# Branch outputs rewritten on gates finished in the projection, with a router on turned tokens and an early start of the first expert

## The reference, cut to what matters

```python
proj = h @ p['w_in'][l] + p['b_in'][l]      # dz and mo are 1024 columns each of it
...
o_dn = o_f + flip(o_b)                      # 8 heads of 128
y_a = (rmsnorm(o_dn, p['dn_onorm'][l]) * jax.nn.silu(dz.reshape(bsz, t, DN_HEADS, DN_DV).astype(f32)))
...
h_ml = h_f + flip(h_b)                      # 4 heads of 256
y_b = rmsnorm(h_ml, p['ml_onorm'][l]) * jax.nn.sigmoid(mo.reshape(bsz, t, ML_HEADS, ML_DV).astype(f32))
y = jax.nn.sigmoid(ga) * (y_a @ p['w_up_a'][l]) + jax.nn.sigmoid(gb) * (y_b @ p['w_up_b'][l])
y = y @ p['w_out'][l]
...
aff = jax.nn.softmax((h @ w_router).astype(jnp.float32), axis=-1)      # 16 experts
gate, idx = lax.top_k(jnp.swapaxes(aff, 1, 2), cap)                    # 16 + 64 tokens each
xe = h[bi, idx]
a = jnp.einsum('becd,edf->becf', xe, w_gate)
u = jnp.einsum('becd,edf->becf', xe, w_up)
ye = jnp.einsum('becf,efd->becd', jax.nn.silu(a) * u, w_down) * gate[..., None].astype(h.dtype)
```

## Time and profile before

| | |
|---|---|
| median of 3 runs | 3671.08 us (3667.51 to 3673.53) |
| the profiled execution | 3677.44 us |
| its span | 3675.6 us |
| mean granted clock of TensorE | 0.953 of full speed |
| projection | 0 to 1391.6 us |
| DeltaNet | 1400.0 to 1755.3 us |
| mLSTM | 1755.8 to 1914.0 us |
| branch outputs | 1915.9 to 1973.5 us |
| merge, without the router tail | 1973.8 to 2454.2 us |
| router tail | 2454.2 to 2522.3 us |
| experts | 2522.6 to 3675.6 us |

### The profile page before, as it was taken

One profiled execution on the slowest core, in us unless ns is written; L12 is line 12 of the kernel. 1 busy time (PEld: TensorE's weight loads), 2 busy tenths in 40 slices (PEclk: granted clock), 3 DMA queues, 4 the chain that ended last, 5 costly groups with the idle time before them and its releaser, 6 DMA issues. The chain is left out here.

```text
span 3675.6 us, 49680 instructions
## 1 busy us (share of the span) xinstructions
PE 3365.8 (92%) x19747; PEld 2764.0 (75%) x19747; DVE 2379.5 (65%) x2580; ACT 1749.4 (48%) x2121; POOL 305.6 (8%) x320
## 2 busy tenths in 40 slices
PE   5899999999999997999665999996999999999994
PEld 0799998888888997889544998874666666666663
DVE  1577456655565664555577334466888888888886
ACT  2444223323323334655323223443777777777774
POOL 0000000000000003241100100000010010010001
PEclk8999999999999998999887999986999999999997
DMA  9322325566663322211342533575999999999997
GB/s 414 132 91 95 125 76 192 206 205 211 208 209 119 113 104 66 69 34 34 81 109 98 176 112 138 217 294 187 372 394 381 399 385 388 399 381 394 397 377 290
DMA packets 181120, 796.74 MB, mean 217 GB/s; under 512 B 17492, under 2 KB 75092, under 8 KB 101604
## 3 DMA queue, kind: packets, MB, share of 16 engines
q1 hardware_dynamic: 162772, 701.71, 51.4%
q0 software_dynamic: 17328, 87.63, 7.1%
q10 hardware_dynamic: 864, 5.27, 0.3%
HBM read 732.10 MB, written 62.46 MB: 216 GB/s over the span
## 5 line engine op out<-in xcount | busy, mean ns | idle before, releaser
L2390 DVE TENSOR_TENSOR expert_lo<-expert_ring,expert_hi 128x2048 fp32r<-128x2048 f32 x384 | 879.4, 2291 | 159.1 <-ACT expert_hi L2327 155.7
L2327 ACT ACTIVATE expert_hi<-expert_ring 128x2048 fp32r<-128x2048 f32 x384 | 735.9, 1917 | 251.2 <-PE bank L2274 228.5
L2272 PE MATMUL bank<-expert_hi,xeT_hi 128*80 128x512 f32 x1024 | 403.8, 394 | 1.2 <-DVE xeT_lo L2395 1.2
L2273 PE MATMUL bank<-expert_lo,xeT_hi 128*80 128x512 f32 x1024 | 402.0, 393 | 0.0
L2274 PE MATMUL bank<-expert_hi,xeT_lo 128*80 128x512 f32 x1024 | 399.2, 390 | 0.0
L451 PE MATMUL bank<-h_hi,part_hi 128*128 128x320 f32 x960 | 302.0, 315 | 6.7 <-DVE part_lo_b L829 3.7
L451 PE MATMUL bank<-h_lo,part_hi 128*128 128x320 f32 x960 | 298.9, 311 | 0.0
L658 ACT ACTIVATE part_hi<-part_x 128x1024 fp32r<-128x1024 f32 x120 | 127.4, 1062 | 247.5 <-PE bank L451 232.8
L1895 ACT ACTIVATE merge_w_hi<-merge_ring 128x2048 fp32r<-128x2048 f32 x48 | 92.0, 1916 | 308.3 <-PE bank L1821 161.5
L829 DVE TENSOR_TENSOR part_lo_x<-part_x,part_hi 128x1024 fp32r<-128x1024 f32 x120 | 147.1, 1226 | 141.1 <-ACT part_hi L658 133.6
L451 PE MATMUL bank<-s_hi,part_hi 128*128 128x320 f32 x720 | 226.7, 315 | 0.0
(11 more groups left out here) (387 smaller groups left out, 7377.9 us busy)
## 6 DMA issues: line engine op xcount, KB each, us to landing
expert_ring<-d_wgate SPq DMA_DIRECT2D x128, 1024.0 KB, 6.8
expert_ring<-d_wup_e SPq DMA_DIRECT2D x128, 1024.0 KB, 7.8
expert_ring<-d_wdown SPq DMA_DIRECT2D x128, 1024.0 KB, 10.4
mod_slot<-d_wmod SPq DMA_DIRECT2D x60, 1024.0 KB, 7.1
part_b<-d_win SPq DMA_DIRECT2D x90, 512.0 KB, 3.6
front_ring<-d_wmod SPq DMA_DIRECT2D x36, 1024.0 KB, 8.1
merge_ring<-d_wout SPq DMA_DIRECT2D x32, 1024.0 KB, 4.9
front_ring<-d_win SPq DMA_DIRECT2D x29, 1024.0 KB, 4.8
```

The lines of the kernel that those rows point to most:

```text
L2272: pe.matmul(out[0:CAP, :], a_hi, hi, start=first, stop=False)
L2273: pe.matmul(out[0:CAP, :], a_hi, lo, start=False, stop=False)
L2327: act.activation(w_hi[n % NSPLIT][:], w[:, n % NSLOT].rearrange("p (k n) -> p k n", n=HALF), ACT.Copy).then_inc(s["we_high"], 1)
L2390: dve.tensor_tensor(w_lo[n % NSPLIT][:], w[:, n % NSLOT].rearrange("p (k n) -> p k n", n=HALF), w_hi[n % NSPLIT][:].bitcast(F32), ALU.subt ...
```

## The change

- In the projection the turn of the late vectors comes one pair later, and so do its copy and store. The tiles of z and o become finished gates before they are stored: ACT applies Silu or Sigmoid to the tile in its row buffer, POOL multiplies by the channel's gain, drains, stores. The last two tiles are stored by SP.
- mLSTM's SP fetches the first steps' tiles before the states, then the states, then the gates (into `z_gate` and `mo_gate`). POOL signals `ready` before it clears `o_ml`. ACT adds, at the end of a step, eight squares with sums of `o_dn`.
- The branch outputs scale `o_dn` on DVE block by block, make squares and scaling of `o_ml` on ACT by head, turn through eight banks, and multiply 128x512 at once by the finished gate; the raster pieces stay 128x128.
- The router's product has the router's columns as the standing and the turned tokens as the moving operand; its result, experts by tokens, is copied and turned back. `h2T` has two buffers, and the order on PE changes. DVE makes the last block's rows before the softmax of group 0.
- ACT splits the first three weight tiles of expert 0 in the tail; the four turns of its rows have a bank each; DVE makes their low parts before that of the fourth weight tile.

The diff, cut to its core:

```diff
-                    if p == VECTOR_PAIR:
+                    if p == VECTOR_PAIR + 1:
                         pe.wait_ge(s["vec_ready"], 1)
...
+                for b in range(2):
+                    sp.wait_ge(s["out_made"], MADE * N_PAIRS - 1 + b)
+                    sp.dma_start(k.d_proj[N_TILES - 2 + b], ob[b][:]).then_inc(k.last_stored, 16)
...
-                for n in range(N_TILES):
+                for n in range(N_TILES - 2):
...
+                    if gate_of(n):
+                        gain = k.chan[:, gate_of(n)[1]:gate_of(n)[1] + 1]
+                        pool.wait_ge(s["gated_out"], n - T_Z + 1)
+                        pool.tensor_tensor(ob[n % 2][:], ob[n % 2][:], gain.to_broadcast([P, T]), ALU.mult)
+                        pool.drain()
                     pool.dma_start(k.d_proj[n], ob[n % 2][:]).then_inc(stored[n % 2], 16)
...
+                    if gate_of(na - 1):
+                        act.activation(ob[1][:], ob[1][:], gate_of(na - 1)[0]).then_inc(s["gated_out"], 1)
                     for j in range(7):
                         m = part_number(p, j) + HI_SLOTS
                         if m < 7 * N_PAIRS:
                             part_high(*divmod(m, 7))
+                        if j == T4 and gate_of(na):
+                            act.wait_ge(s["out_made"], MADE * p + 6)
+                            act.activation(ob[0][:], ob[0][:], gate_of(na)[0]).then_inc(s["gated_out"], 1)
...
+                for d in range(2):
+                    fetch(d, 0)
                 for d in range(2):
                     sp.dma_start(S[1][d][:, :, 0:DV_ML], k.d_smc[d].rearrange("h p n -> p h n")).then_inc(state_in, 16)
...
+                for g, t0 in ((k.z_gate, T_Z), (k.mo_gate, T_MO)):
+                    sp.dma_start(g[:], k.d_proj[t0:t0 + 8].rearrange("m p t -> p m t")).then_inc(gates_in, 16)
...
+                pool.drain().then_inc(s[0]["ready"], 1)
                 pool.memset(k.o_ml[:], 0.0)
-                pool.drain().then_inc(s[0]["ready"], 1)
+                pool.drain().then_inc(o_zeroed, 1)
...
+                    for h in range(H_DN):
+                        act.activation(square[:, h, :], col(k.o_dn[:], tiles[0], h * P, (h + 1) * P), ACT.Square,
+                                       accum_out=col(k.dn_ms[:], tiles[0], h, h + 1))
...
+                act.activation(dn_rs[:], k.dn_ms[:], ACT.Sqrt, bias=k.eps, scale=1.0 / P).then_inc(dn_rooted, 1)
+                for t in range(TT):
+                    for h in range(H_ML):
+                        act.activation(square[:, t, h, :], k.o_ml[:, t, h * DV_ML:(h + 1) * DV_ML], ACT.Square,
+                                       accum_out=ml_ms[:, t, h:h + 1])
...
+                            op = dve.tensor_tensor(y[:, cs, tokens], src, g[:, cs, tokens], ALU.mult)
...
-                            mm = pe.matmul(k.bank[t // 3][:, t * N_EXP:(t + 1) * N_EXP], hT[:, kk, :], wr[:, kk, :],
-                                           start=(kk == 0), stop=(kk == KT - 1))
+                            mm = pe.matmul(out, wr[:, kk, :], hT[t % 2][:, kk, :], start=(kk == 0), stop=(kk == KT - 1))
...
+                scale_x1(4)
+                shift(4)
                 subtract_max(0)
-                scale_x1(4)
                 normalise(0)
-                shift(4)
...
+                for n in range(EARLY_SPLIT):
+                    high_expert(n)
...
+            return (k.bank[5], k.bank[6], k.bank[7], k.bank[3])[r] if e == 0 else k.bank[5]
```

More of the change, by code:

```diff
@@ L1047, in _ @@
                 sp.wait_ge(k.rows_out, 16)
[L1048 to L1049 removed]
+                sp.wait_ge(k.last_stored, 32)
                 sp.wait_ge(prompt_done, 4)
@@ L1383, in _ @@
                                      ).then_inc(state_in, 16)
[L1385 to L1392 removed]
+                for g, t0 in ((k.z_gate, T_Z), (k.mo_gate, T_MO)):
+                    sp.dma_start(g[:], k.d_proj[t0:t0 + 8].rearrange("m p t -> p m t")).then_inc(gates_in, 16)
+                with sp.Fori(0, TT - 1) as i:
+                    for d, tile in enumerate((i + 1, i * -1 + (TT - 1))):
+                        bank[d]["A"].wait_filled(sp, i, "NP3")
+                        fetch(d, tile)
+                sp.wait_ge(gates_in, 32)
                 sp.wait_ge(prompt_done, 1)
@@ L1609, in phase_branch_outputs, with bank @@
-        o = [k.o_dn, k.o_ml]
-        heads = [H_DN, H_ML]
+        square = sb("ml_square", [P, TT, H_ML, DV_ML])
+        ml_ms = sb("ml_ms", [P, TT, H_ML])
+        dn_rs, ml_rs = sb("dn_rs", [P, TT, H_DN]), sb("ml_rs", [P, TT, H_ML])
+        dn_rooted, ml_rooted, ml_rs_made, dn_scaled, ml_scaled, turned, read = (k.sem("bo_" + n) for n in (
+            "dn_rooted", "ml_rooted", "ml_rs_made", "dn_scaled", "ml_scaled", "turned", "read"))
+        BANKS = 8
+        def bank(b, t, half):
+            return k.bank[(2 * TT * b + 2 * t + half) % BANKS]
@@ new lines, in _ @@
+                dve.wait_ge(dn_rooted, 1)
+                dve.reciprocal(dn_rs[:], dn_rs[:])
+                dve.drain()
+                scale_dn(0)
+                for t in range(TT):
+                    if t + 1 < TT:
+                        scale_dn(t + 1)
+                    gate(0, t)
+                    if t == 2:
+                        dve.wait_ge(ml_rooted, 1)
+                        dve.reciprocal(ml_rs[:], ml_rs[:])
+                        dve.drain().then_inc(ml_rs_made, 1)
@@ L1647, in _ @@
+                for t in range(TT):
+                    gate(1, t)
+            @block.tensor
+            def _(pe):
+                for b, (o, scaled) in enumerate(((k.o_dn, dn_scaled), (k.o_ml, ml_scaled))):
                     for t in range(TT):
+                        pe.wait_ge(scaled, t + 1)
                         for half in range(2):
-                            bank = k.bank[n % 6]
-                            dve.wait_ge(turned, n + 1)
+                            n = 2 * TT * b + 2 * t + half
+                            if n >= BANKS:
+                                pe.wait_ge(read, n - BANKS + 1)
@@ L1665, in _ @@
[L1665 to L1681 removed]
+                                mm = pe.transpose(bank(b, t, half)[:, j * P:(j + 1) * P], o[:, t, c * P:(c + 1) * P],
@@ L1857, in route, with logits @@
                         mm.then_inc(s["turned"], 1)
+                def logits(t):
+                    out = logits_bank(t)
                     for b in range(4):
@@ L1878, in _ @@
                 pe.wait_ge(s["wr_in"], 16)
-                for t in range(TT - 1):
-                    route(t)
+                turn_h(0)
+                turn_h(1)
+                logits(0)
+                turn_h(2)
+                logits(1)
+                logits(2)
+                turn_h(3)
+                turn_logits(0)
+                logits(3)
+                turn_h(4)
+                logits(4)
                 turn_affinities(0)
-                route(TT - 1)
+                turn_logits(1)
                 turn_affinities(1)
@@ L2253, in turn_x @@
                         pe.wait_ge(s[f"xe_landed{b % 2}"], i * 16 + (16 * (b // 2) + 16))
-                    if isinstance(i, int) and 8 * i + 4 * b + r > 0 or not isinstance(i, int):
+                    first = isinstance(i, int) and 8 * i + 4 * b == 0
+                    if not first:
                         pe.wait_ge(s["x_low"], i * 8 + (4 * b + r))
@@ L2412, in _ @@
                     x_low(0, r)
+                for n in range(EARLY_SPLIT, NSPLIT):
+                    low(n)
                 for e in range(N_EXP):
```

196 lines of the change are left out of this document (99 added, 97 removed).

## The result

The changed kernel takes 3614.05 us (median of 4 runs, 3611.75 to 3617.62) against 3672.31 us for the kernel before on the same chip, a ratio of 0.9841 with a 95% interval of 0.9826 to 0.9855: 58 us less, with 53 to 64 inside the interval. The forecast was 3604.7, the range 3593 to 3627.

| stretch | before | after | difference | forecast |
|---|---|---|---|---|
| projection, to DVE's last combination | 1391.56 | 1385.49 | -6.1 | -9.0 |
| from there to the next block's first DVE instruction | 8.48 | 0.82 | -7.7 | -6.7 |
| DeltaNet | 355.8 | 356.0 | +0.2 | 0 |
| mLSTM, to the branch outputs | 160.1 | 155.0 | -5.0 | -4.5 |
| branch outputs, to the merge | 57.9 | 25.1 | -32.9 | -29.3 |

A forecast was written before the change was run, and what follows sets the result against it. TensorE was busy 92% of the span, with waits on serial chains between bulk matmuls. Gains 9.0 + 0 + 6.7 + 4.5 + 29.3 + 9.9 + 7.0 = 66.4 us gave 3604.7 us on the median's scale, range 3593 to 3627.

The forecast's parts named there:

- Transpose: Projection: turning the late vectors one pair later removes TensorE's 7.4 us wait and half-clock excess behind it; gain 9.0 us.
- Finished gates at 0: Projection: gate work on ScalarE and POOL in eight pairs costs 0 us, at worst 8.
- The named cover of 1.8 us: First buffer of a gate pair: store lands at 907.2, ScalarE overwrites at 908.98; this 1.8 us covers the later store.
- Last stores on SP: Projection's end: moving the last two stores from POOL to SP removes most of the 7.61 us gap; gain 6.7 us.
- the rival of a gap that has nothing to do with it: Projection's end: the 7.61 us gap comes from the block's size or end and stays; 3611 us, chance 0.17.
- mLSTM: mLSTM's start: fetching the first tiles before the states brings the first matmul sooner; gain 4.5 us.
- Branch outputs: Branch-output stage: less VectorE work, squares on ScalarE beside it, 28.3 us in place of 57.6; gain 29.3 us.
- 1.8 us for turns between engines: Branch outputs: allowance added to VectorE's 26.5 us for turns between engines, giving 28.3 us.
- Router tail: Router tail: moving 128 columns keeps the clock at 1.00, so the last choice starts sooner; gain 9.9 us.
- The rival of a half clock: Router tail: the clock stays at 0.50, the choice starts 9.6 us later than today; 3624 us, chance 0.17.
- First expert: First expert block: early ScalarE splits and separate banks cut start to first matmul from 17.0 to 10 us; gain 7.0.
- POOL as pacer: Projection's gate pairs: long drains after stores make POOL set the pace, 77 us at 19 us a tile; 3682 us, chance 0.02.

The follow-up runs named there:

- e7: Changed kernel with the projection's last two tiles stored by POOL again and POOL waiting until both have landed: 3621.30 us.
- e4: Changed kernel with the router product's operands as before (16 router columns moving, no copy and turn back of the logits): 3635.44 us.
- e9: Changed kernel with expert weight loads held until the first rows land, VectorE's low parts held and reordered, a small POOL product before the gates: 3611.42 us, ratio 0.9843.
- e1: Changed kernel with expert weight loads behind the first eight held on SP until the first expert's rows have landed: 3610.63 us.
- e10: Changed kernel without any edit, run again beside e9 on the same chip: 3615.08 us, ratio 0.9853.
- e5: Changed kernel with one more product and drain on POOL, on zeros, at the very start of the program: 3616.16 us.
- e2: Changed kernel with VectorE's three low parts of expert 0 held until POOL's counter, meant to follow the first gather's issue: 3614.21 us.

## Why the prediction was right, point by point

- **Transpose:** right, 9.9 us against 9.0. The wait and the half clock behind it went together, and nothing was late next.
- **Finished gates at 0:** the step that failed. Their sum used the product's 1.6 us and the store's 2.4 us, and neither held in the first pair: 2.24 + 3.89 us on POOL, and then 7.3 us to the landing beside SP's loads, so that ACT waited 7.83 us. The named cover of 1.8 us was gone. That the price, 7 us over all traces, lies inside the 8 that it gave is luck: the step had slow products in every pair, where it was one drain in the first, and by its own numbers even POOL's slowest product (2.4 us) has the store landed at 908.0, 1 us ahead of the overwrite.
- **Last stores on SP:** right, 7.7 us (6.7). e7 shows the cause to the extent that a store on POOL brings the gap back; so the rival of a gap that has nothing to do with it falls.
- **mLSTM:** right, 5.0 us (4.5).
- **Branch outputs:** the mechanism was right, the size 32.9 us against 29.3. Two terms were mis-sized. The raster products took 0.28 us each where 0.337 was taken from the old fused product, 1.8 us of the 3.6. The 1.8 us for turns between engines were hardly needed, since ACT's squares were done (1907.0) when DVE was at its third block; the other terms came out 0.4 above the sum, and 0.3 is the old stage counted from ACT's start to the next block's (57.9 for 57.6).
- **Router tail:** right, 11.4 us (9.9), and e4 shows the reason, the operands. The rival of a half clock did not come; e4, whose tail did run at 0.50, came out 17.1 us later, near the 19.5 that the rival was given.
- **First expert:** the sum's second failure, 2.5 us for 7.0, under its lower end of 4. The step counted what ACT and DVE were spared and took the landing of the rows (6.16 us) as given. It was 10.86: the work that was moved forward fell on the gather, DVE's low parts beside POOL's issue (2.1 us, e9 against e1) and weight loads beside its bytes (2.5 us, e1).
- **The sum:** by the places the change gives 9.9 - 7 + 7.7 + 5.0 + 32.9 + 11.4 + 2.5 = 62.4 us, inside the 53 to 64 of the medians, where 66.4 was forecast. The gates' 7 us and the expert's 4.5 went one way, branch outputs, tail, border, transpose and mLSTM, 7.5 us, the other. That 66.4 nearly met the 65.7 of the two profiled executions is luck too: 4 of the 65.7 lay ahead of pair 5, where no edited instruction had run.
- **POOL as pacer:** it did not come. A gate tile occupies POOL for 2.5 to 3.5 us of its 14.2, the first for 6.7.
- **The signs that it named:** one of the wrong ones came, ScalarE waiting for POOL's store, in the first gate pair alone. Of the right ones two did not: the branch outputs took 25.1 us, under the 27 to 31, and the first expert's matmul came 14.5 us in and not 10.

## What to carry to other kernels

Work that is moved forward into an idle stretch should be checked against what issues there. Here a gather on POOL beside VectorE's subtractions of two SBUF tensors took three times as long, and the loads that those subtractions set free ran beside its bytes; delaying VectorE, and the loads with it, by 1.6 us gained 4.0. A block's border, and the first product behind a run of stores on POOL, have prices of their own (7.6 and 3.9 us here), which a small edit moves to another queue or to idle time. In a serial tail of small matmuls the choice of the moving operand can decide the clock: with 128 columns moving it stayed at 1.00 and 32 instructions took 3.67 us, with 16 it fell to 0.50 and they took 6.85.

## What the runs showed of the hardware that was not expected

- POOL's drain behind its first product after a run of stores took 3.89 us in all eight traces of the gates as changed, and 0.65 to 0.67 us behind the others; a small product and drain 25 us earlier took it off, one at the start of the program did not.
- A gather's issue on POOL took 0.96 us with VectorE idle and 1.86 to 3.03 us beside VectorE's 128x2048 subtractions, and ended some 0.9 us behind the end of the one under way. POOL's product of 128x640 had two prices in the same manner, 1.24 us and, begun 0.10 us behind a subtraction, 2.24; a plain store's issue did not (0.54 us).
- In the gate pairs a store of 320 KB landed in 2.4 to 2.5 us when SP's load of 1 MB came behind it, and in 5.5 to 8.4 us when SP issued one beside it or up to 3 us ahead of it (changed kernel, e9 and e10).
- A block's border behind a store on POOL took 7.61 us from the end of its issue with the store left under way, and 5.12 with its landing waited for, against 0.82 us behind VectorE's last combination with no store on POOL.
- The projection up to pair 5, in which no program here differs but for e5's one product and a small memset in e9, took 724 to 731 us from execution to execution. The merge without its tail took 481.2 to 481.8 us in nine of the twelve traces and 484.7 to 484.9 in three (e2, e4, e10), and the changed kernel itself has both (481.4 and, in e10, 484.7).
